# Delta rule: the second pair's units beside the first pair's levels, and no products on a zero state

## The reference

```
a_kk = where(strict, (k * beta) @ k.T * decay, 0)
t_inv = inverse(eye + a_kk)
u = t_inv @ (v * beta);  w = t_inv @ (k * beta * exp(gcum))
qk = (q @ k.T) * decay;  q_dec = q * exp(gcum);  k_dec = k * exp(gcum[-1] - gcum)
```

```
v_new = u - w @ state
o = q_dec @ state + qk @ v_new
state = state * g_tot + k_dec.T @ v_new
```

## Time and profile before

| what | value |
|---|---|
| runs | 3318.32, 3318.49, 3320.39 us, median 3318.49 |
| the profiled execution | 3314.17 us, its span 3312.4 us |
| TensorE (PE) busy | 3156.4 us, 95% of the span |
| DVE, ACT, POOL busy | 57%, 43%, 13% |
| mean granted clock of TensorE | 0.991 |
| first mixed stage, both units and chains | about 144 to 477 us |

### The profile page before, as it was taken

One profiled execution on the slowest core, in us unless ns is written; L12 is line 12 of the kernel. 1 busy time (PEld: TensorE's weight loads), 2 busy tenths in 40 slices (PEclk: granted clock), 3 DMA queues, 4 the chain that ended last, 5 costly groups with the idle time before them and its releaser, 6 DMA issues.

```text
span 3312.4 us, 60366 instructions
## 1 busy us (share of the span) xinstructions
PE 3156.4 (95%) x25968; PEld 2502.3 (76%) x25968; DVE 1875.3 (57%) x3082; ACT 1411.3 (43%) x2478; POOL 426.7 (13%) x444
## 2 busy tenths in 40 slices
PE   8899899999998989999999998999999989999999
PEld 5677777888876677778888876767788767676887
DVE  6666657666466665656746565563544555535443
ACT  5645223433346434333423345554433456444432
POOL 0051430000000230510000000121301001204010
PEclk9899999999999999999999999999999999999999
DMA  5001113333333001123333333212132232122223
GB/s 174 26 17 46 40 34 109 104 96 97 98 103 96 21 22 53 31 69 104 97 98 96 92 106 118 74 46 70 57 92 73 87 112 94 45 67 61 77 80 99
DMA packets 80218, 255.06 MB, mean 77 GB/s; under 512 B 11344, under 2 KB 13008, under 8 KB 78928
## 3 DMA queue, kind: packets, MB, share of 16 engines
q1 hardware_dynamic: 79952, 251.19, 24.9%
HBM read 238.08 MB, written 6.29 MB: 74 GB/s over the span
## 4 chain that ended last, share of the span: by engine, by line
PE 77%; DVE 9%; ACT 7%; POOL 3%; issue 2%; DMA 1%; SPq 1%; POOLq 0%; ACTq 0%; DVEq 0%
PE psum L534 74%; PE psum L710 2%; POOL s_xb L2686 2%; DVE s_xb L1971 2%; DVE s_wlo L1971 1%; ACT s_tmp L1267 1%; ACT s_whi L1267 1%; DVE s_tmp L1974 1%; DMA s_stage<-w 1%; ACT s_E L1267 1%; POOL s_tmp L2686 1%; DVE s_ffy L1974 1%; SPq L2820 0%; ACT L1267 0%; ACT L1277 0%
## 5 line engine op out<-in xcount | busy, mean ns | idle before, releaser
L534 PE MATMUL psum<-s_h,s_whi 128*128 128x512 f32 (+1 forms) x4576 | 1453.8, 399 | 11.8 <-DVE s_wlo L1971 6.7
L534 PEld LDWEIGHTS psum<-s_h,s_whi 128*128 128x128 f32 (+1 forms) x4576 | 846.4, 188 | 222.4 <-issue 29.8
L534 PE MATMUL psum<-s_h,s_wlo 128*128 128x512 f32 (+1 forms) x2288 | 895.7, 391 | 0.0
L1971 DVE TENSOR_TENSOR s_wlo<-s_stage,s_whi 128x1024 fp32r<-128x1024 f32 (+2 forms) x468 | 526.1, 1127 | 373.3 <-ACT s_whi L1267 372.3
L1267 ACT ACTIVATE s_whi<-s_stage 128x1024 fp32r<-128x1024 f32 (+2 forms) x468 | 450.0, 966 | 280.9 <-DMA s_stage<-w 82.7
L534 PEld LDWEIGHTS psum<-s_h,s_wlo 128*128 128x128 f32 (+1 forms) x2288 | 429.9, 188 | 94.7
L534 PE MATMUL psum<-s_ffa,s_whi 128*128 128x512 f32 x704 | 217.6, 390 | 4.6 <-DVE s_ffa L1971 4.6
L2718 POOL TENSOR_SCALAR s_E<-s_E,s_inv,s_g 128x128 f32<-128x128 f32 (+3 forms) x128 | 76.6, 608 | 1054.1 <-DVE s_inv L2079 1034.2
L2686 POOL TENSOR_TENSOR s_xb<-s_xb,s_cstm 64x512 f32<-64x512 f32 x64 | 90.4, 1412 | 909.2 <-DVE s_xb L1971 904.8
L1974 DVE SCALAR_TENSOR_TENSOR s_ffy<-psum,s_pcol,s_ffy 128x511 f32<-128x511 f32 x176 | 131.7, 748 | 110.8 <-ACT s_ffy L1267 107.7
L1267 ACT ACTIVATE s_E<-psum,s_nm 128x256 f32<-128x256 f32 (+3 forms) x224 | 114.3, 515 | 174.0 <-DVE s_nm L2057 138.6
(11 more groups left out here) (307 smaller groups left out, 4407.8 us busy)
## 6 DMA issues: line engine op xcount, KB each, us to landing
s_stage<-w SPq DMA_DIRECT2D x192, 512.0 KB, 3.6
s_stage<-wup SPq DMA_DIRECT2D x88, 512.0 KB, 3.6
s_stage<-wo SPq DMA_DIRECT2D x32, 512.0 KB, 3.6
s_stage<-wdn SPq DMA_DIRECT2D x32, 512.0 KB, 3.5
s_stage<-wdn SPq DMA_DIRECT2D x16, 384.0 KB, 3.1
spill<-s_x SPq DMA_DIRECT2D x2, 2048.0 KB, 9.4
s_stage<-woa SPq DMA_DIRECT2D x16, 256.0 KB, 2.6
s_x<-spill SPq DMA_DIRECT2D x2, 2048.0 KB, 7.8
```

The source lines that it names most:

```text
L534: return self.e.matmul(out, left, right, start=first, stop=last, skip_group_check=True)
L1971: return self.e.tensor_tensor(out, a, b, op)
```

## The change

Pair 1's units start ten turns after pair 0's instead of after its end, on tiles of their own: the second half of `wT`, S, two halves of `kdec`, a new tile `more`, and a tile of `early` or `rope`. `kdec` is then made by POOL in halves, late in pair 1. The units take 27 turns in place of 34. The turns of the plugs are new: of 18 halves 6, 8, 4 and 0 were in units 0, chain 0, units 1 and chain 1, and now 6, 8, 0 and 4 are. The fill of g=1 goes one turn for one. Banks of `g` and `gq` are put back two turns later, those of `kq` after the transposes. The chain leaves out the w and q products at s=0 and the k product, the decay and the state's sum at s=7; the first state is a copy of the k product, and S isn't cleared.

```
@@ -267,18 +267,21 @@
-        units = lambda g: abreast(self.units(l, g, 0), self.units(l, g, 1))
         fill = itertools.chain(attention(), project(1, (0, 1)))
         beside(abreast(scalars, begun, delayed(project(0, (1,)), 0)), fill, 1, 1)
-        beside(plugged(units(0), plug, (0, 1, 4, 5, 21, 22)), fill, 1, 1)
-        beside(plugged(self.chain(l, 0), plug, (2, 3, 6, 7, 10, 11, 14, 15)), fill, 1, 1)
+        beside(plugged(self.units(l, 0), plug, (0, 1, 4, 5, 14, 15)), fill, 1, 1)
+        beside(plugged(self.chain(l, 0), plug, (0, 1, 4, 5, 8, 9, 12, 13)), fill, 1, 1)
         for _ in fill:
             pass
         fill = gates()
-        beside(plugged(units(1), plug, (4, 5, 21, 22)), fill, 5, 4)
-        beside(self.chain(l, 1), fill, 5, 4)
+        beside(plugged(self.units(l, 1), plug, ()), fill, 1, 1)
+        beside(plugged(self.chain(l, 1), plug, (0, 1, 4, 5)), fill, 1, 1)
         for _ in fill:
             pass
+
+    def units(self, l, g):
+
+        return abreast(self.unit(l, g, 0, 0), self.unit(l, g, 0, 1), delayed(self.unit(l, g, 1, 0), 10), delayed(self.unit(l, g, 1, 1), 10))
...
-                    self.S, self.xb = sd("S", [128, 2, 2, 128]), sd("xb", [128, 10, T])
+                    self.S, self.xb, self.more = sd("S", [128, 2, 2, 128]), sd("xb", [128, 10, T]), sd("more", [128, T])
...
-        self.slot = [[self.xb[:, 5 * n + i, :] for i in range(5)] for n in range(2)]
+        pairs = self.kdec[:, :, :, :].rearrange("p r (h i) d -> p r h (i d)", h=2)
+        zero = self.S[:, :, :, :].rearrange("p r j d -> p (r j d)")
+        later = lambda g: (self.early2[:, 5, :], self.rope[:, 0, :])[g]
+        self.slot = [[[[self.xb[:, 5 * r + i, :] for i in range(5)] for r in range(2)],
+                      [[self.wT[:, r, 1, :], (zero, self.early2[:, 6, :])[r], pairs[:, r, 1 - r], (self.more[:, :], later(g))[r], pairs[:, r, r]] for r in range(2)]] for g in range(2)]
...
-        X, Y, Pm, A, AT = m.slot[r]
+        X, Y, Pm, A, AT = m.slot[g][jp][r]
...
         last.then_inc(*self.up("pe_unit", key, "gq"))
+        yield
+        yield
         self.give((key, "g"), ("vec_unit", key, "gd"))
         self.give((key, "gq"), ("act_unit", key, "D"))
-        yield
-        yield
         if r == 0:
...
             last.then_inc(*self.up("pe_unit", both, "kq"))
-            for e in range(2):
-                self.give((both, "kq", e), *[("vec_unit", (l, g, jp, s), "q", e) for s in range(2)])
         yield
         yield
         ps = self.take((key, "AT"))
         self.w.wait_ge(*self.at("vec_unit", key, "A", 1))
         self.eight(ps, A, None, True).then_inc(*self.up("pe_unit", key, "AT"))
+        yield
         self.give((key, "AT"), ("act_unit", key, "AT"))
-        yield
+        if r == 1:
+            for e in range(2):
+                self.give((both, "kq", e), *[("vec_unit", (l, g, jp, s), "q", e) for s in range(2)])
         yield
         for b in range(1, 6):
...
                 pr, cs = slice(64 * a, 64 * a + 64), slice(i * 128 + 64 * a, i * 128 + 64 * a + 64)
+                if s == 0:
+                    continue
                 self.w.wait_ge(*self.at("vec_chain", key, "S", s - 1, r))
...
-                if s > 0:
-                    self.w.wait_ge(*self.at("act_chain" if s <= 4 else "vec_chain", key, "o", s - 1, 1 - r))
+                if s == 0:
+                    continue
...
             for r in range(2):
+                if s == 7:
+                    continue
+                if s in (0, 4):
+                    self.w.wait_ge(*self.at("pool_unit", (l, g, 1, r), "kdec", r if s == 0 else 1 - r))
                 i, a = place(s, r)
                 pr = slice(64 * a, 64 * a + 64)
-                self.w.wait_ge(*self.at("vec_chain", key, "v", s, r))
+                if s > 0:
+                    self.w.wait_ge(*self.at("vec_chain", key, "v", s, r))
...
-                self.w.wait_ge(*self.at("pe_chain", key, "q", s, r))
+                if s > 0:
+                    self.w.wait_ge(*self.at("pe_chain", key, "q", s, r))
+                if s == 7:
+                    self.w.wait_ge(*self.at("vec_chain", key, "v", s, r))
                 for jp, e in heads:
                     hd, at = slice(64 * (2 * jp + e), 64 * (2 * jp + e) + 64), (4 * e + i) * 64
-                    last = self.mm(self.bank((key, "o", e))[pr, jp * 64:jp * 64 + 64], m.M2[pr, r, jp, at:at + 64], m.u[pr, r, i, hd], False, True)
+                    last = self.mm(self.bank((key, "o", e))[pr, jp * 64:jp * 64 + 64], m.M2[pr, r, jp, at:at + 64], m.u[pr, r, i, hd], s == 0, True)
...
-                self.give((key, r, e), ("vec_chain", key, "S", 7, r))
+                self.give((key, r, e), ("vec_chain", key, "v", 7, r))
...
-        for r in range(2):
-            self.e.memset(m.S[:, r], 0.0).then_inc(*self.up("vec_chain", key, "S", -1, r))
         for s in range(8):
-            for r in range(2):
+            for r in range(2 if s > 0 else 0):
                 i, a = place(s, r)
                 pr = slice(64 * a, 64 * a + 64)
                 us = heads(m.u[pr, r, i, :])
                 self.w.wait_ge(*self.at("pe_chain", key, "w", s, r))
                 self.tt(us, us, each(m.psum[pr, banks[r]:banks[r] + 2, 0:128]), ALU.subtract).then_inc(*self.up("vec_chain", key, "v", s, r))
             yield
-            for r in range(2):
+            for r in range(2 if s < 7 else 0):
+                if s == 0:
+                    self.w.wait_ge(*self.at("pe_chain", key, "k", s, r))
+                    self.e.tensor_copy(m.S[:, r, :, 0:64], two(m.psum[:, banks[r], 128:256])).then_inc(*self.up("vec_chain", key, "S", s, r))
+                    continue
...
-        if jp == 1:
+
+        def decayed(n):
             heads = lambda a: a.rearrange("p i (h e) -> p i h e", h=4)
-            hs = slice(8 * r + 4 * g, 8 * r + 4 * g + 4)
+            hs, i2 = slice(8 * r + 4 * g, 8 * r + 4 * g + 4), slice(2 * n, 2 * n + 2)
             self.w.wait_ge(*self.at("act_proj", (l, "p", g, 1, 1), "tok"))
             self.w.wait_ge(*self.at("act_dn", (l, "bd"), "kd"))
-            self.tt(heads(m.kdec[:, r]), heads(m.ktok[g][:, :, :]), B(sc["kd"][:, hs, :].rearrange("p c i -> p i c")[:, :, :, None], 3, 64), ALU.mult).then_inc(*self.up("pool_unit", key, "kdec"))
-            self.last = "pool_unit", key, "kdec"
+            self.w.wait_ge(*self.at(*self.last))
+            self.tt(heads(m.kdec[:, r, i2]), heads(m.ktok[g][:, i2, :]), B(sc["kd"][:, hs, i2].rearrange("p c i -> p i c")[:, :, :, None], 3, 64), ALU.mult).then_inc(*self.up("pool_unit", key, "kdec", n))
+            self.last = "pool_unit", key, "kdec", n
...
-        for jp in range(2):
-            yield from self.unit(l, g, jp, r)
+            elif jp == 1:
+                decayed(r)
+            yield
+            yield
+        if jp == 1:
+            self.w.wait_ge(*self.at("pe_unit", key, "Y", 5))
+            decayed(1 - r)
+        yield
...
-        for s in range(8):
+        for s in range(1, 7):
```

More of the change, by code:

```diff
@@ L1670, in unit @@
         yield
-    def units(self, l, g, r):
-        for jp in range(2):
-            yield from self.unit(l, g, jp, r)
     def chain(self, l, g):
```

17 lines of the change are left out of this document (6 added, 11 removed).

## The result

The changed kernel takes 3332.01 us, the median of six runs (3326.83 to 3333.6), beside 3318.87 for six runs of the kernel before: a ratio of 1.0034, 95% interval 1.0022 to 1.0045. It is slower by 0.34%, some 13 us, where 3310.0 was forecast; the time lies above the range. The profiled execution has a span of 3331.6 us and a mean clock of 0.986. It took 1.4 us more than the median, while the profiled execution of the kernel before, 3314.17, took 4.7 less than its own, so the two profiles show more than the medians do: 19 us instead of 13.

A forecast was written before the change was run, and what follows sets the result against it. TensorE was taken as the bound, busy 3156.4 of 3312.4 us. Per-layer terms -0.7 + 4.1 + 3.3 - 5.0 - 2.8 + 4.5 + 0.85 = 4.25, 8.5 in all, took 3318.5 to 3310.0 us; range 3295 to 3326.

The forecast's parts named there:

- chain(0) and chain(1): The chains' products, state clearing and plugs: 3.3 us a layer gained in chain(0), 0.85 in chain(1).
- Second head of g=0 ... Gain 4.1: Second pair's head beside the first pair's levels: 9.3 us of waits and slow clock gone, 5.2 new, a layer.
- Queue on DVE: Rival: head passes on DVE delay subtractions and bank-freeing copies, so heads wait as long as before; 3327.2 us, chance 0.18.
- Instruction supply: Rival: denser 64x64 products bring more unexplained PE waits, +6 us, 3316; chance 0.30 together with the tail-only rival.
- The end of chain(0): Last convolution of v stands bare behind the chain: wait 5.6 and slow clock 1.5, less 2.1 gone; 5.0 us a layer lost.
- First head of g=1: First pair's head in g=1 loses its plugs, 14 groups of linear matmuls instead of 18: 2.8 us a layer lost.
- Second head of g=1 ... Gain 4.5: Second pair's head in g=1: 6.0 us of waits and 1.5 of slow clock gone, 3.0 of new waits, a layer.
- First head of g=0: First pair's head in g=0: `kq` banks wait for one DVE copy, 0.7 us a layer lost.
- Second heads without waits of 2 us and more: Sign in the changed profile: second pairs' heads have no such waits, except level 4 of lane 1 in g=0.
- `s_xb` near 32.8: Sign that the forecast is wrong: PE's total waits for `s_xb` on DVE stay near their earlier 32.8 us.

The follow-up runs named there:

- e1: The kernel before with only the change's chain edits; units, tiles, plugs and fills stay: 3304.22 us, ratio 0.9956.
- e3: The changed kernel with the six DVE operations that begin the second pair's head one turn later, behind the attention copy: 3327.09 us, ratio 1.0027.
- e12: The changed kernel with two of chain(0)'s half linears moved behind the chain, into the last convolution of v: 3324.99 us, ratio 1.0015.
- e2: The changed kernel with the fill going three steps for two turns in chain(0): 3343.82 us, ratio 1.0071.
- e10: The change with the overlap in g=0 only, fill five steps for four turns beside the units, chain(0)'s plugs one turn later: 3321.51 us, ratio 1.0003.
- e6: The changed kernel with the overlap in g=1 only; g=0's units one after the other with their old plugs: 3309.48 us, ratio 0.9969.
- e8: e1 with the two DVE passes of k times beta moved from the first level to the third: 3293.01 us, ratio 0.9919.
- e9: e1 with the fill of g=0's units slowed to three steps for four turns, no overlap: 3324.70 us, ratio 1.0013.

## Why the prediction was wrong

By its own steps, per layer, against e1 (the change's chains without its order).

**chain(0) and chain(1): right in kind.** The wait for `s_S` is gone and 96 products fewer run. Of the 4.15 forecast for both, 0.86 (1.96 - 1.1) was for the plugs that cover the q products and some 3.3 for the edits themselves. e1, which has the edits alone, measured 4.4 by its stages and more by its medians. The cover of the q products turned out smaller: the q waits of 1.96 became waits of 0.87 and three of 0.20 for the plugs' banks, 1.47, where 1.1 was taken.

**"Second head of g=0 ... Gain 4.1": this step failed.** The waits to be removed were removed. The new ones were put at 4.4; they are 7.83 in the six rows and 2.62 at the end of pair 1, 10.45 in all, against 7.83 in the head that stands apart in e1 (the five waits of the earlier trace rows, within a few hundredths). So the six waits took the place of the five at the same price, by chance to the hundredth, and 2.62 is lost on top; layer 1 reads the same, 10.46 against 7.80, with a second stretch at the low clock. Waits for nothing that the profile shows are longer too, 1.4 us against 0.65 in layer 0 and 1.9 against none in layer 1. A gain of 4.1 became a loss of 2.6 in waits for engines, and of 3.3 to 4.5 with these.

The one wait that was worked out from the order, level 4 of lane 1, came out right: 2.6 forecast, 2.91 measured. The others were taken at one short pass each. Level 3 was put at 0.6 for an ACT pass and 0.6 for a subtraction, and waited 1.70 and 0.88; level 5 was put at 0.6 and waited 1.60. There the bank is that of an attention score, which comes back only when DVE's maximum and ACT's exponential have gone through. With pair 1's `g` and `gq` of both lanes open for two turns more, four of the eight banks are held, and in the program's order the list is down to two or three at level 3, where before has six or seven, so a product takes a bank that has just been used. Followed through that order, all six waits are for a bank: 3.81 us of them behind ACT's exponentials, 3.14 behind DVE's attention copies and 0.88 behind a subtraction. The 2.62 was missed altogether: the last levels of the second pair have neither another pair nor, at u, a linear beside them.

*Queue on DVE* was the rival nearest in size (3327.2, still 4.8 below the time measured), and its condition held: new waits above 12.45 a layer, with 10.45 here and 6.33 in g=1. Its mechanism is only half of it: e3 took DVE's passes out of the way, and the wait went to the next bank. How much shorter these waits would be with another order of DVE's passes was not tried beyond that. *Instruction supply* fits a small part: the waits for nothing shown went from 5.7 to 7.2 us in all, 1.5 where it had 6, and no run shows what they are.

In all, g=0 takes 8.7 us a layer more than in e1 (7.2 and 10.2). By the rows some 3.7 of it are the tail's waits, 2.6 the second head's, 1.3 waits for nothing shown there and 1.4 slower products; the covered q products give back 0.5.

The Trainium skill, "Perfetto Trace Analysis", Matmul Optimizations, asks that all eight PSUM banks be leveraged to maximize the available instruction-level parallelism. Going by it, four units in the eight banks should have filled the gaps. The trace shows the other side: with the list nearly empty, 1.70 and 1.60 us of waiting stand at products whose inputs were ready. The Trainium skill, "Trainium Kernel Development and Optimization", Best Practices, with its word on PSUM pressure, was nearer, and the forecast had it only as a reason for the upper bound.

**"The end of chain(0)": right place, too small.** The wait was put at 5.6 and is 5.88. The clock was put at 1.5 and takes 2.5. That can be read from the same products in e12, where the clock is up: from the start of the last transposes to the first linear behind them the change takes 7.21 us (357.59 to 364.80) and e12 4.73.

```profile
364.80 0.73 PE L541 MATMUL psum<-s_h,s_whi 128*128 128x512 f32 x2
...
355.10 0.60 PE L629 MATMUL psum<-s_cst,s_tmp 128*128 128x128 f32 x4
...
359.83 0.73 PE L542 MATMUL psum<-s_h,s_whi 128*128 128x512 f32 x2
```

2.0 of the 2.5 fall behind the boundary of g=1, and are the part of its loss that e2, e10 and e12 don't have. With the waits of 1.35 and 0.78 gone, 5.88 - 2.13 + 2.5 makes some 6.2, where 5.0 was forecast.

**First head of g=1: right, as far as it can be read.** 2.8 were forecast. Its waits are 6.46 (1.81, 3.71, 0.94) against 5.16 in e1 (2.23, 1.11, 1.82), and there are two stretches at the low clock (379.5 to 387.0 at a mean of 0.54) instead of one: 1.3, and a fall of the clock, which is 1.5 by the forecast's own price and was not measured by itself.

**"Second head of g=1 ... Gain 4.5": failed too.** Of 3.0 for new waits there are 6.33 (0.89, 0.21, 0.45, 1.75, 3.03), against 4.49 in e1 (2.08, 2.41), with one stretch at the low clock fewer. In layer 0 waits for nothing shown are 2.9 us against 0.3. That is nothing gained, as e6 says for the group. The 3.03 is a wait for a bank as well. Six were in the list, but a product takes the first one, and that was the bank of the first pair's `w`. It came back late by DVE's fixed order: its subtraction waited 2.53 for POOL's block, then came a weight pass of 2.28, and only then the copy that frees the bank:

```profile
435.26 0.69 DVE L1982 TENSOR_TENSOR s_early<-s_cstm,s_early 128x512 f32<-128x512 f32 x1 [2.53 <-POOL s_early L2695]
435.87 2.28 DVE L1982 TENSOR_TENSOR s_wlo<-s_stage,s_whi 128x1024 fp32r<-128x1024 f32 x1
438.08 0.74 DVE L2348 COPY s_wT<-psum 128x256 f32<-128x256 f32 x2
```

**First head of g=0**: 0.7 forecast, 0.93 for `s_ktok` measured, but e1's 1.43 at the next product shrinks away, so about nothing.

**The signs named in advance.** The wait for `s_S` and the 96 products came as said; so did the 5 to 6 us ahead of the last transpose. "Second heads without waits of 2 us and more" did not hold: 3.03 in g=1, and 2.62 at the end of pair 1 in g=0. And "`s_xb` near 32.8" was the wrong mark to watch: it fell by 13.1, in part by the new names of tiles, while four other rows rose by more. It would have needed the sum over all releasers of these products.

## What to carry to other kernels

When the main part of an interleaved order gets shorter, the fill beside it does not: count the turns on both sides first, since what is left stands bare behind the last one, and covering it from elsewhere uncovers something else (e2, e10, e12). Before two parts are put side by side, write out for each product who last used its bank; a wait on an input is easily traded for a wait on a bank. And look first, on the engine that ends a wait, for a pass whose result nobody wants yet: moving two such passes (e8) gave 11 us, more than the 8.5 forecast for the whole change.

## What the runs showed of the hardware

The two passes of k times beta took 3.42 us in e1, beside POOL's block passes (242.06 to 247.73 us), and 1.29 at their new place in e8, where POOL's next pass begins only at 260.08, on the same shapes (259.40 to 260.69). In the changed kernel the one slow pass of the head, 1.75 beside five of about 0.68, runs beside POOL's too (208.88 to 210.49). So moving a pass can also make it shorter. The Trainium skill, "SBUF — State Buffer", section "SBUF: two separate sides", says that DVE and POOL share a pair of ports, which one holds for a whole instruction when DVE has two SBUF inputs and POOL's instruction reads SBUF; these rows agree with it.

The low clock outlives a wait. Through the end of the 5.88 us in the changed kernel and the products behind it, 355.6 to 363.2, the granted clock is 0.55 in the mean, and it is the same around the 5.79 in e9. So the price of a long wait is the wait and, here, 2.5 us on the work behind it, where the fall after the 3.27 of the earlier trace rows was taken for 1.5. But not every wait of 3 us is followed by a fall. After the 3.01 in g=1 of e6 the granted clock stays at 1.00 (first row), and after the same wait of 3.03 in the change it is 0.50 (second):

```profile
429.85:433.30 3.45, 3.45 (x134) 3.01 (x134) 3.45 (x5) 0.00 (x0) 2.33 (x2) 1.00 0.02 5
438.20:441.60 3.40, 2.97 (x112) 3.00 (x116) 3.40 (x5) 0.00 (x0) 2.76 (x2) 0.50 0.03 5
```

So the forecast's way to price the clock, by whether a wait is 2.2 us and more, doesn't hold in these runs.

Waits for nothing that the profile shows come and go between kernels with the same matmuls: 4.9 us in e1, 10.5 in e8, with up to 2.7 in one place. They were not explained.
